# Products without a reader on TensorE in the odd layer of a two-layer encoder: six in the wait for the norm, two behind the second key scores, one behind each of five levels of a triangular inverse

## The reference, cut to what matters

```
kk = jnp.einsum('bhntd,bhnsd->bhnts', kc, kc)
m = jnp.where(strict, betac[..., :, None] * kk * gam, 0.0)
...
sol = lax.linalg.triangular_solve(m + jnp.eye(CHUNK, dtype=F32), rhs, left_side=True,
                                  lower=True, unit_diagonal=True)
u, w = sol[..., :C_DV], sol[..., C_DV:]
qk = jnp.einsum('bhntd,bhnsd->bhnts', qc, kc) * gam
```

## Time and profile before

| what | value |
|---|---|
| median of three runs | 582.05 us (580.44 to 582.09) |
| the profiled execution's own time | 584.52 us |
| its span, first to last instruction | 582.6 us |
| mean granted TensorE clock | 0.926 of full speed |
| busy: TensorE, VectorE, ScalarE, GpSimd | 543.8, 286.7, 250.9, 82.7 us |
| TensorE's share of the chain that ended last | 77% |

### The profile page before, as it was taken

How to read it: one execution, slowest core, us unless ns; L and a number is a source line. 1 busy time by engine, 2 the same in 40 slices (tenths; PEclk the granted TensorE clock), 3 DMA queues, 4 the chain that set the end, 5 groups by cost and what they waited for, 6 DMA issues and landing times.

```text
span 582.6 us, 11397 instructions
## 1 busy us (share of the span) xinstructions
PE 543.8 (93%) x4818; PEld 462.5 (79%) x4818; DVE 286.7 (49%) x538; ACT 250.9 (43%) x495; POOL 82.7 (14%) x101
## 2 busy tenths in 40 slices
PE   6999999999999999879999997999998989999985
PEld 6999999996576665479989997999998956656642
DVE  3669988657111121348995466464255571122113
ACT  5676587663142332335556233300334734323311
POOL 5715730100000000021005700011020000000000
PEclk9999999997899999979999799655599999999999
DMA  8991335689899999986544330000041999999994
GB/s 317 287 354 45 109 110 158 239 341 397 315 410 409 394 410 407 367 271 218 168 159 147 111 109 1 1 3 2 2 145 54 406 410 399 408 409 409 409 405 161
DMA packets 56853, 143.83 MB, mean 247 GB/s; under 512 B 4468, under 2 KB 29264, under 8 KB 56800
## 3 DMA queue, kind: packets, MB, share of 16 engines
q1 hardware_dynamic: 55648, 141.62, 64.8%
q0 software_dynamic: 976, 1.38, 1.2%
q10 hardware_dynamic: 176, 0.07, 0.1%
HBM read 142.00 MB, written 1.05 MB: 246 GB/s over the span
## 4 chain that ended last, share of the span: by engine, by line
PE 77%; DVE 7%; DMA 6%; ACT 4%; issue 3%; SPq 2%; ACTq 0%; DVEq 0%
PE PS L2178 9%; PE PS L645 7%; PE PS L647 6%; PE PS L646 6%; PE PS L2139 6%; DMA XD<-moe_w_down 6%; PE PS L2203 3%; PE PS L681 3%; PE PS L683 3%; PE PS L682 3%; PE PS L2564 3%; PE PS L2576 3%; PE PS L2214 2%; PE PS L2215 2%; PE PS L2055 2%
## 5 line engine op out<-in xcount | busy, mean ns | idle before, releaser
L645 PE MATMUL PS<-WH,HTH 128*128 128x384 f32 (+2 forms) x272 | 90.6, 333 | 3.1 <-DVE HTL L1349 1.4
L641 DVE TENSOR_TENSOR WL<-RAW,WH 128x768 fp32r<-128x768 f32 (+2 forms) x84 | 76.5, 946 | 30.2 <-ACT WH L622 29.9
L647 PE MATMUL PS<-WH,HTL 128*128 128x384 f32 (+2 forms) x272 | 88.1, 324 | 0.0
L646 PE MATMUL PS<-WL,HTH 128*128 128x384 f32 (+2 forms) x272 | 88.1, 324 | 0.0
L1357 DVE SCALAR_TENSOR_TENSOR HID<-SIL,MW,PS 128x128 f32<-128x128 f32 x18 | 6.2, 347 | 127.0 <-ACT SIL L1033 127.0
L622 ACT ACTIVATE WH<-RAW 128x768 fp32r<-128x768 f32 (+2 forms) x84 | 63.1, 797 | 4.1 <-PE PS L647 2.1
L645 PEld LDWEIGHTS PS<-WH,HTH 128*128 128x128 f32 x272 | 51.9, 191 | 4.4 <-DVE HTL L1349 1.6
L646 PEld LDWEIGHTS PS<-WL,HTH 128*128 128x128 f32 x272 | 51.9, 191 | 0.0
L647 PEld LDWEIGHTS PS<-WH,HTL 128*128 128x128 f32 x272 | 51.7, 190 | 0.0
L1033 ACT ACTIVATE SIL<-PS,MW 128x128 f32<-128x128 f32 x18 | 6.6, 368 | 94.7 <-PE PS L2178 84.2
L681 PE MATMUL PS<-HTH,WH 128*128 128x256 f32 x160 | 46.2, 289 | 0.0
(11 more groups left out here) (366 smaller groups left out, 1136.0 us busy)
## 6 DMA issues: line engine op xcount, KB each, us to landing
RAW<-moe_w_down SPq DMA_DIRECT2D x32, 512.0 KB, 14.0
RAW<-moe_w_gate SPq DMA_DIRECT2D x28, 512.0 KB, 6.9
RAW<-moe_w_up SPq DMA_DIRECT2D x28, 512.0 KB, 8.5
RAW<-od_w_in SPq DMA_DIRECT2D x9, 1536.0 KB, 7.0
XD<-moe_w_down SPq DMA_DIRECT2D x24, 512.0 KB, 13.9
XG<-moe_w_gate SPq DMA_DIRECT2D x24, 512.0 KB, 9.0
XG<-moe_w_up SPq DMA_DIRECT2D x24, 512.0 KB, 10.3
RAW<-ev_w_in SPq DMA_DIRECT2D x5, 1536.0 KB, 13.3
```

What stands on the lines that cost most here:

```text
L641: done(nc.vector.tensor_tensor(out=lo, in0=raw, in1=hi.bitcast(F32), op=ALU.subtract), "unit_lo")
L645: nc.tensor.matmul(ps, ah, bh, start=start, stop=False)
L646: nc.tensor.matmul(ps, ah, bl, start=False, stop=False)
L647: return nc.tensor.matmul(ps, al, bh, start=False, stop=stop)
```

## The change

`filler(n)` is new: n float32 products of the identity with 512 columns of the constant table, into bank 0, without a wait and without a reader. Six of them take the place of the ten of `warm(10)` ahead of the odd layer's norm; two stand behind `key_scores(1)`; one stands behind each of the inverse's levels one to five. Nothing else moves, on no engine.

```diff
+            def filler(n):
+                for _ in range(n):
+                    mm(PS[:, 0, :], ident, CT[:, C_DEC:C_DEC + 512], start=True, stop=True)
+
             def in_projection(layer, n, between):
                 if layer:
-                    warm(10)
+                    filler(6)
                 norm_T(layer, 0)
...
             key_scores(1)
+            filler(2)
             retention_scores(1)
             pe.wait_ge(sem("c_nt"), 3)
             for L in range(1, 7):
...
                 inverse_Z(0, L)
                 inverse_Z(1, L)
+                if L < 6:
+                    filler(1)
                 if L == 2:
                     values_T()
                 if L >= 3:
```

## The result

The changed kernel takes 560.55 us (median of four runs, 558.91 to 564.24) against 581.25 us before (four runs, 579.04 to 582.09): a ratio of 0.9658, 95% interval 0.9601 to 0.9716, some 20 us. The forecast of 580.5 us and its range, 566 to 586.5, were wrong. The rival of the held clock had 560.5 us.

A forecast was written before the change was run, and what follows sets the result against it. TensorE, at half clock in the inverse's levels, was taken to bound the kernel. Terms of -2.7, 0, +0.2, +7.0 and -6.0 sum to -1.5 us, taken from the median of 582.05: 580.5 us, range 566 to 586.5.

The forecast's parts named there:

- The rival of the held clock: Inverse's levels: the fillers hold full clock throughout, 560.5 us in all; chance 0.14.
- A, the start: Ahead of the odd layer's norm: six fillers for ten warm products fill the gap and hold the clock, -2.7 us.
- B, the key fillers: Behind the second key scores: two fillers run in time before VectorE's matrix is ready, 0 us, at most +0.8.
- C, level one's filler: Behind level one: 0.86 us of filler in TensorE's wait of 0.64 us for VectorE's transpose, +0.2 us.
- D and E: Levels: four fillers behind two to five cost +7.0 us; returns of full clock behind one to five give -6.0.
- the 2.5 returns: Stretches regaining full clock: one behind level one, one behind two, half the time behind three to five; -6.0 us together.
- The first fall: Ahead of the levels, clock 0.82 to 0.50: put behind TensorE waits of 0.95 and 0.80 us and only small products.
- Rival 1: Inverse's levels: a filler for each level holds full clock throughout, -18.8 us there, 560.5 us in all; chance 0.14.
- its partial form: Clock held over part of the levels, two or three returns more than counted: 573 to 578 us; chance 0.19.
- Rival 2: Levels two to five: small products lose the clock at once, fillers cost and buy nothing, +4.5, 586.5 us; chance 0.13.

The follow-up runs named there:

- the repeated measurement: Six fillers at the start alone, none behind key scores or levels, against the kernel before, with twelve executions: 577.2 us against 581.39, ratio 0.9926.

## Why the prediction was wrong

- **What bounds.** Right: TensorE, at half clock in the levels, with VectorE busy for half of the time; and the gain reached the end.
- **A, the start.** Right, and somewhat small: -2.4 us forecast up to the first projection product and -0.4 for the six records from there, -2.8 and -0.4 by the trace, together -3.3 for the -2.7 taken; -4.3 us (2.6 to 5.9) by the repeated measurement. The gap ended when forecast.
- **B, the key fillers.** Right at 0 for the place that it priced: from the first retention score to the inverse's first product it is 5.01 us before (355.74 to 360.75) and 5.04 after (351.14 to 356.18). Whether they bring a us or two in the retention outputs behind, the runs without them can't tell.
- **C, level one's filler.** Its direct cost was right and beside the point. From level one's Z to the next Q it is 2.70 us before and 3.04 after, +0.3. The term priced only the filler's time, and this filler alone brings 20 us.
- **D and E, the step that failed.** The sentence "So it is not idle time alone: the small products don't hold the clock" drew one conclusion from two facts. The forty us at 0.50 without a gap show that small products don't bring the clock back. They don't show that small products lose a full one. What lost it was the wait behind level one at full clock: filled by a product of 512 columns, full-width or narrow, or of 256, the clock stays; left open by the same product in another place, it falls; left half open (128 columns), it fell in the traced execution, and six of seven took 587 us or more. The four fillers at 1.75 us and the 2.5 returns at 2.4 us never came up; both together had +1.0, and the trace shows -18.4 us from level one's Z on (-15.4 and -3.0). The price of the half clock was low as well: 64 small products cost 3.60 - 2.06 = 1.54 us more by the rows, not 1.4 or 1.45.
- **The first fall** pointed at waits too. The prediction listed 0.95 and 0.80 us ahead of it and left out the last and longest, 1.15 us, in the kernel before; PEclk is 1.00 from 361 to 363 and falls within the two us behind that wait (0.59 and 0.50):

```profile
363.02 1.82 PE L2564 MATMUL PS<-XC,NTD 64*64 64x32 f32 x32 [1.15 <-DVE XC L1892]
```

- **Rival 1** was right that the clock is held and right in size: -18.8 us against the -18.4, a level at 5.9 us against 5.77 measured, and VectorE near: 16.74 busy in 20. That each level needs its filler, as it had it, was wrong: one does. I gave it 0.14, and 0.33 with its partial form. The rule of the Trainium skill (TensorE: Matmul & The Clock Gate, "Why this matters for your kernels"), that gaps lose the full rate, pointed the right way. But the gaps that the page warns of are longer than this one, so it wouldn't have picked out a wait of 0.64 us, which sufficed here beside narrow products; the measurement decides. What the page says of the way back, that continuous work brings it, is not what these rows show for 64x64 products: TensorE was busy for 45.00 of 45.00 us at 0.50.
- **Rival 2** has kernels with its time, the filler ahead of Z and most executions with 128 columns, but not its mechanism: the small products don't lose the clock as soon as they begin, as the changed kernel's 20.00 us at PEclk 1.00 show.
- The fillers behind levels two to five cost what they take: 3.6 us by the traces, 560.55 against 556.64 us by the medians. What they bought in these runs is the return after a loss behind level one, which the first filler prevents.

Open: why the clock comes back later behind the first rows in the kernel with the filler ahead of Z (near 434 us, for 425 before), why one kernel with 128 columns has two outcomes, and how the kernel before would fare if the wait were shortened on VectorE instead.

## What to carry to other kernels

Where the granted clock is low for long, look at the last turn down, not at the low stretch: what runs there may be able to hold the full clock and only unable to bring it back, and one product in one short wait ahead of it was worth 20 us here. Try the product in the wait and the same product beside it; the pair tells waits from columns. Then take out each filler that isn't needed, since on the bound engine it costs its time.

## What the runs showed that I hadn't expected

- Levels made up mostly of 64x64 products of 32 columns kept PEclk at 1.00 for twenty us (four calls of 32 records each level, 2.06 us for 64) and stayed at 0.50 for over forty us in the same order (3.60 us for 64). In these stretches the clock stayed as it was found.
- Waits of 0.64 us, and of 0.23 and 0.24 us together (one trace; by the times six of seven executions), decided between them; a wait of 0.28 us three levels later, or a single one of 0.21 to 0.24 us in level one, with the narrow product or with 256 columns, didn't lose the clock.
- The end of the gap behind the branch lay some 6 us (5.87 to 6.23) behind the first product after it, whether TensorE stood or ran 5.4 us of fillers in it.
